# Recurrence outputs with high and low part side by side, and earlier sums in the down projection, in a two-block transformer kernel

## What is computed

```
def hgrn2_recurrence(q, k, v, log_f):
    """S_t = diag(f_t) S_{t-1} + k_t v_t^T,  o_t = S_t^T q_t, chunkwise."""
    ...
    q_in = q * jnp.exp(b)
    ...
    scores = jnp.einsum('nbhtk,nbhsk->nbhts', q_in, k_in)
    scores = jnp.where(causal, scores, 0.0)
    o_intra = jnp.einsum('nbhts,nbhsv->nbhtv', scores, v)
    def step(state, inp):
        o_inter = jnp.einsum('bhtk,bhkv->bhtv', q_n, state)
    ...
    o = o_intra + o_inter
...
    o = rms_norm_2(o, hg_norm_g)
    o = o * jax.nn.silu(hz).reshape(B, S, HG_HEADS, HG_DIM)
```

## Time and profile before

| what | value |
|---|---|
| three runs | 1290.31, 1290.8, 1291.3 us; median 1290.8 |
| the profiled execution, its own time | 1290.74 us |
| its span in the profile | 1288.9 us |
| PE busy | 1279.2 us (99%), 6297 matmuls |
| DVE, ACT, POOL busy | 726.0, 689.4, 498.9 us |
| granted clock of PE | 0.999 over the span |
| DMA | 132.32 MB, 103 GB/s on average |

### The profile page before, as it was taken

One profiled execution on the slowest core, in us unless ns is written; L12 is line 12 of the kernel. 1 busy time (PEld: TensorE's weight loads), 2 busy tenths in 40 slices (PEclk: granted clock), 3 DMA queues, 4 the chain that ended last, 5 costly groups with the idle time before them and its releaser, 6 DMA issues.

```text
span 1288.9 us, 16219 instructions
## 1 busy us (share of the span) xinstructions
PE 1279.2 (99%) x6297; PEld 1073.6 (83%) x6297; DVE 726.0 (56%) x1321; ACT 689.4 (53%) x1031; POOL 498.9 (39%) x207
## 2 busy tenths in 40 slices
PE   9999999999999999999999999999999999999998
PEld 7888888888887888888888888888878888888886
DVE  6656556552138456565768377777656556642442
ACT  5535544543235657666447577777655545462422
POOL 4553433434444332322335534434333333334530
PEclk9999999999999999999999999999999999999999
DMA  5732332324332232332243322222223222225411
GB/s 176 274 119 95 91 98 86 103 87 164 98 101 95 86 105 69 98 97 65 66 160 99 115 82 66 82 82 66 82 82 101 72 88 74 91 99 204 163 57 66
DMA packets 42589, 132.32 MB, mean 103 GB/s; under 512 B 6992, under 2 KB 9744, under 8 KB 42000
## 3 DMA queue, kind: packets, MB, share of 16 engines
q1 hardware_dynamic: 36416, 115.36, 28.0%
q10 hardware_dynamic: 6096, 15.92, 3.5%
HBM read 124.97 MB, written 10.49 MB: 105 GB/s over the span
## 4 chain that ended last, share of the span: by engine, by line
PE 93%; DVE 4%; ACT 1%; DMA 1%; issue 1%; POOL 0%; SPq 0%; DVEq 0%; ACTq 0%
PE banks L509 28%; PE banks L511 28%; PE banks L510 28%; PE banks L716 2%; PE banks L708 1%; PE banks L697 1%; DVE ylo L1748 1%; DMA raw<-w 1%; PE banks L623 1%; PE banks L936 1%; DVE nfull L1744 1%; ACT whi L1097 0%; PE banks L968 0%; PE banks L967 0%; DVE acc L1612 0%
## 5 line engine op out<-in xcount | busy, mean ns | idle before, releaser
L499 POOL TENSOR_TENSOR wlo<-raw,whi 128x1024 fp32r<-128x1024 f32 (+2 forms) x198 | 487.9, 2466 | 718.2 <-ACT whi L1097 717.8
L509 PE MATMUL banks<-hhi,whi 128*128 128x512 f32 x736 | 292.9, 398 | 0.2 <-DVE hlo L1795 0.2
L511 PE MATMUL banks<-hlo,whi 128*128 128x512 f32 x736 | 287.2, 390 | 0.0
L510 PE MATMUL banks<-hhi,wlo 128*128 128x512 f32 x736 | 287.1, 390 | 0.0
L1097 ACT ACTIVATE whi<-raw 128x1024 fp32r<-128x1024 f32 (+2 forms) x198 | 205.3, 1038 | 148.8 <-PE banks L511 86.7
L509 PE MATMUL banks<-yhi,whi 128*128 128x512 f32 x464 | 182.8, 394 | 0.7 <-ACT mcg L1471 0.5
L511 PE MATMUL banks<-ylo,whi 128*128 128x512 f32 x464 | 180.9, 390 | 0.0
L510 PE MATMUL banks<-yhi,wlo 128*128 128x512 f32 x464 | 180.7, 389 | 0.0
L511 PEld LDWEIGHTS banks<-hlo,whi 128*128 128x128 f32 x736 | 138.2, 188 | 29.3
L509 PEld LDWEIGHTS banks<-hhi,whi 128*128 128x128 f32 x736 | 138.5, 188 | 25.4 <-DVE hlo L1795 1.0
L510 PEld LDWEIGHTS banks<-hhi,wlo 128*128 128x128 f32 x736 | 138.6, 188 | 24.5
(11 more groups left out here) (389 smaller groups left out, 2177.4 us busy)
## 6 DMA issues: line engine op xcount, KB each, us to landing
raw<-w SPq DMA_DIRECT2D x193, 512.0 KB, 3.5
rel_tab<-relx ACTq DMA_DIRECT2D x1, 4096.0 KB, 19.5
tab<-rel_tab SPq DMA_DIRECT2D x16, 224.0 KB, 3.5
x<-xt ACTq DMA_DIRECT2D x1, 2048.0 KB, 8.7
x_kept<-x ACTq DMA_DIRECT2D x1, 2048.0 KB, 7.4
parts_kept<-mcg SPq DMA_DIRECT2D x8, 256.0 KB, 4.3
mgt<-parts_kept SPq DMA_DIRECT2D x8, 256.0 KB, 3.7
x<-x_kept ACTq DMA_DIRECT2D x1, 2048.0 KB, 8.3
```

The source lines that it names most:

```text
L499: nc.gpsimd.tensor_tensor(lo[:, begin:width], raw[:, n % 2, begin:width], f32(hi[:, begin:width]), ALU.subtract).then_inc(lo_done, 1)
L509: nc.tensor.matmul(dst, a[0], b[0], start=first, stop=False)
L510: nc.tensor.matmul(dst, a[1], b[0], start=False, stop=False)
L511: return nc.tensor.matmul(dst, a[0], b[1], start=False, stop=last)
```

## The change

In the recurrence's outputs the moving operand gets both parts: `hss` and `hqbs` hold for each block 128 high and beside them 128 low columns. A product with the high part of the stationary operand now moves 256 columns, one with the low part 128. An output block so has 256 columns of PSUM, the low-part product apart from the rest; the four blocks take bank 3 and bank 5. New steps add the two up: on ACT `hg_low` copies the low columns (two instructions, 128x256) into `hb`, a tile that is free then, and on DVE `hg_sum` adds the high columns to it (two instructions). What read bank 3 reads `hb`. As bank 5 is taken until `sum`, the score blocks come in the order 1, second half of 3, 0 (behind a wait for `sum`), first half of 3 and 2.

In the down projection the banks are dealt anew, the squares of tiles 0 to 2 stand before `hg_root(7)` on ACT, the others behind it; `down_sums` is laid between the tiles of `dn 5` instead of `g0 0`, and DVE's rotation comes after the means, half of it after the diagonal matrix.

```
-DN_BANK = (1, 0, 2, 5, 4)
+DN_BANK = (1, 0, 2, 4, 6)
...
-            hqbs = [sb(n, [P, 2, TT - 1, P], F32R, scope) for n in ("hqbhi", "hqblo")]
+            hqbs = sb("hqbs", [P, 2, TT - 1, 2, P], F32R, scope)
...
-            hss = [sb(n, [P, S], F32R, scope) for n in ("hshi", "hslo")]
+            hss = sb("hss", [P, TT, 2, P], F32R, scope)
...
+        out_pairs = [bank[3 if t < 2 else 5][:, (t % 2) * 2 * P:(t % 2 + 1) * 2 * P] for t in range(TT)]
+        out_split = [bank[b].rearrange("p (t c v) -> p t c v", c=2, v=P) for b in (3, 5)]
+        hb_parts = [hb[:, i * 2 * P:(i + 1) * 2 * P].rearrange("p (t v) -> p t v", v=P) for i in range(2)]
...
# PE
+                if k == 4:
+                    pe.wait_ge(hpV.sem, hpV.at("qlo", s))
+                    if s >= 1:
+                        pe.wait_ge(htV.sem, htV.at("far1", s - 1))
+                    hg_block(s, 1)
+                if k == 5:
+                    hg_block(s, 3, slice(CROSS, CROSS + P))
+                if k == 6:
+                    if s >= 1:
+                        pe.wait_ge(hoV.sem, hoV.at("sum", s - 1))
+                    hg_block(s, 0)
+                if k == 7:
+                    hg_block(s, 3, slice(0, CROSS))
+                    if s >= 1:
+                        pe.wait_ge(mzA.sem, mzA.at("z", s - 1))
+                    hg_block(s, 2).then_inc(htP.did("scores"), 1)
...
-                last = mm3(bank[3][:, cols], [u[:, s, t, :] for u in hv], [u[:, cols] for u in hss], True, t == 0)
+                nc.tensor.matmul(to, hv[0][:, s, t, :], hss[:, t, :, :], start=True, stop=False)
+                last = nc.tensor.matmul(to[:, 0:P], hv[1][:, s, t, :], hss[:, t, 0, :], start=False, stop=t == 0)
...
+                    nc.tensor.matmul(to, hsts[0][:, t - 1, :], hqbs[:, s % 2, t - 1, :, :], start=False, stop=False)
+                    last = nc.tensor.matmul(to[:, 0:P], hsts[1][:, t - 1, :], hqbs[:, s % 2, t - 1, 0, :], start=False,
+                                            stop=True)
...
+            def down_sums(k):
+                if k not in (2, 3, 6, 7):
+                    return
...
+                if k == 6:
+                    pe.wait_ge(dnV.sem, dnV.at("k1"))
...
+            slab("dn", 5, bank[5], h, between=down_sums)
...
# ACT
+            def hg_low(u):
+                act.wait_ge(htP.sem, htP.at("o", u))
+                act.wait_ge(hpV.sem, hpV.at("four", min(u + 1, HH - 1)))
+                if u >= 1:
+                    act.wait_ge(hoV.sem, hoV.at("norm", u - 1))
+                for got, to in zip(out_split, hb_parts):
+                    low = nc.scalar.activation(to, got[:, :, 1, :], ACT.Copy)
+                low.then_inc(hoA.did("low"), 1)
...
-                act.wait_ge(htP.sem, htP.at("o", u))
-                nc.scalar.activation(ho[:, 0, :], bank[3], ACT.Square).then_inc(hoA.did("sq"), 1)
+                act.wait_ge(hoV.sem, hoV.at("sum", u))
+                nc.scalar.activation(ho[:, 0, :], hb[:, :], ACT.Square).then_inc(hoA.did("sq"), 1)
...
                 if u >= 0:
+                    hg_low(u)
+                cut()
+                if u >= 0:
                     hg_square(u)
-                cut()
...
# DVE
+            def hg_sum(u):
+                dve.wait_ge(hoA.sem, hoA.at("low", u))
+                for got, to in zip(out_split, hb_parts):
+                    last = V.tensor_tensor(to, got[:, :, 0, :], to, ALU.add)
+                last.then_inc(hoV.did("sum"), 1)
...
+                if r >= 1:
+                    hg_sum(r - 1)
                 dve.wait_ge(hpA.sem, hpA.at("qbhi", r))
...
+            down_add("k1", QL, QL + 1)
...
             dve.wait_ge(dnP.sem, dnP.at("tok"))
...
             V.reciprocal(rt3[:, 1, :, :], rt3[:, 0, :, :]).then_inc(dnV.did("inv"), 1)
+            V.tensor_tensor(mt1[:, 0, :], bank[5], mm[:, 1, :], ALU.mult).then_inc(dnV.did("turn"), 1)
+            crossed(dnV, bank[5], (0, 1))
...
                             ALU.mult).then_inc(dnV.did("diag"), 1)
+            crossed(dnV, bank[5], (2, 3))
+            turned_sum(dnV)
```

More of the change, by code:

```diff
@@ L380, in build @@
         hoP = steps("ho_pe", ["ms"], HH)
-        hoA = steps("ho_act", ["sq", "sqhi", "ln", "root"], HH)
-        hoV = steps("ho_dve", ["sqlo", "norm", "y", "yhi", "ylo"], HH)
+        hoA = steps("ho_act", ["low", "sq", "sqhi", "ln", "root"], HH)
+        hoV = steps("ho_dve", ["sum", "sqlo", "norm", "y", "yhi", "ylo"], HH)
         mzA = steps("mz_act", ["z"], HH)
@@ L842, in hg_outputs @@
                     return
[L843 to L844 removed]
+                t, to = k // 2, out_pairs[k // 2]
                 if t == 0:
@@ L895, in _ @@
             slab("dn", 2, bank[2], h, between=lambda k: hg_outputs(s, k))
-            slab("dn", 3, bank[5], h)
+            slab("dn", 3, bank[4], h)
             hg_square(s)
-            slab("dn", 4, bank[4], h)
-            pe.wait_ge(hoV.sem, hoV.at("norm", s))
-            slab("dn", 5, bank[3], h)
+            slab("dn", 4, bank[6], h)
+            def down_sums(k):
+                if k not in (2, 3, 6, 7):
+                    return
+                g, first = k // 4, 2 * (k % 2)
+                if k == 2:
+                    pe.wait_ge(hoA.sem, hoA.at("ln", s))
+                    pe.wait_ge(dnV.sem, dnV.at("q2"))
+                if k == 6:
+                    pe.wait_ge(dnV.sem, dnV.at("k1"))
+                for b in (first, first + 1):
+                    tok = nc.tensor.matmul(bank[3][:, g * TT + b:g * TT + b + 1], dsq[:, (0, QL)[g], b * P:(b + 1) * P],
+                                           ones[:, 0:1], start=True, stop=True)
+                if k == 7:
+                    tok.then_inc(dnP.did("tok"), 1)
+            slab("dn", 5, bank[5], h, between=down_sums)
             def ml_project(r):
@@ L969, in ml_scores @@
                 last.then_inc(msP.did("s"), 1)
[L971 to L983, removed]
             pe.wait_ge(mzA.sem, mzA.all())
-            slab("g0", 0, bank[7], h, between=down_sums)
+            slab("g0", 0, bank[7], h)
             pe.wait_ge(dnV.sem, dnV.at("diag"))
-            for g, b in enumerate((6, 3)):
-                wide = nc.tensor.matmul(bank[b], ones, ddiag[:, g, :], start=True, stop=True)
-            wide.then_inc(dnP.did("wide"), 1)
+            nc.tensor.matmul(bank[3], ones, ddiag[:, 0, :], start=True, stop=True)
+            pe.wait_ge(dnV.sem, dnV.at("sum"))
+            nc.tensor.matmul(bank[5], ones, ddiag[:, 1, :], start=True, stop=True).then_inc(dnP.did("wide"), 1)
             pe.wait_ge(mcA.sem, mcA.at("gate", 0))
```

75 lines of the change are left out of this document (33 added, 42 removed).

## The result

The changed kernel takes 1294.72 us (median of 8 runs, 1293.83 to 1297.24), the kernel before 1290.85 us (median of 8 runs beside them, 1290.26 to 1291.48). The ratio is 1.0033, 95% interval 1.0023 to 1.0043. The forecast was 1294.4 us, slower by more than 0.2%.

The account below looks back on a forecast made before the run. PE bounds the kernel before; the change makes a loop of ACT and DVE, 28.7 us a round, bind instead. 1290.74 + 3.3 (recurrence) + 0.4 (down projection) = 1294.4 us, 8-in-10 range 1285.2 to 1296.8.

Parts of the forecast that it names:

- PE's saving: Recurrence output blocks: each product saves 0.10 us, 0.70 us a round, 5.6 us in eight.
- Rival 4: 256 columns cost as much as twice 128, only the 0.7 is lost: 1295.1 us; 0.08 together with Rival 3.
- rival 2: The loop closes nearly where it was, 0.2 us or less a round longer: 1291 to 1292 us; chance 0.14.
- The chain of ACT and DVE: Recurrence loop without PE, from qlo through adds, square and mzg to the next qlo: 27.3 us becomes 28.7.
- PE's two waits: Each recurrence round, PE waits for qlo at k = 4 (some 0.4 us) and mzg at k = 7 (some 0.8).
- No PE wait in them: From the first masked copy to the next qlo, 22.46 us, ACT and DVE never wait for PE.
- Sum over the rounds: Recurrence up to the last hg_square: six times 0.6, plus 0.37, less 0.70, so +3.3 us instead of -5.6.
- The tail: Down projection: sum ends at 964.65 against 964.26, and pa 0 waits for ACT's gate behind it: +0.4 us.
- Rival 3: dn 5: POOL delays DVE's yhi, ylo and k1, PE waits at its sums: 1296.7 us; 0.08 together with Rival 4.
- Rival 1: Recurrence loop stays under 27.42 us, PE stays the bound and keeps 5.6 us less 0.4: 1285.5 us; chance 0.18.

Follow-up runs that it names:

- load_shift: Changed kernel with Ln and Exp from one table and each weight's copy on ACT one slab later; 1286.50 us, ratio to before 0.9968.
- extra_before: Kernel before, with the high part of the square written twice each round (one more ACT copy); 1290.70 us, ratio 0.9998.
- extra_after: Changed kernel, with the high part of the square written twice each round (one more ACT copy); 1299.79 us, ratio 1.0072.
- load_after: Changed kernel with hg_root's Ln and Exp from one table, one table load less a round; 1294.82 us, ratio to before 1.0031.
- shift_only: Changed kernel with one weight's copy dropped in round 0 and added in round 8, so copies handle the slab before; 1293.39 us, ratio to before 1.0023.
- best: load_shift plus hz and mzg ahead of the square and the gate of g0 0 ahead of sum's high part; 1283.82 us, ratio to before 0.9945.
- mz_cut: mz_first with the weight's copy ahead of the forget gate moved behind it; 1298.43 us, ratio to before 1.0055.
- mz_first: Changed kernel with ACT's gates hz and mzg ahead of the square; 1290.77 us, ratio to before 0.9997.
- mz_load_cut: mz_cut with hg_root's Ln and Exp from one table as well; 1289.92 us, ratio to before 0.9994.
- rec_only: Changed kernel with the down projection's order in ACT, DVE and PE put back, the recurrence's change alone; 1294.17 us, ratio to before 1.0024.
- gate_first: Changed kernel with ACT's gate of g0 0 ahead of sum's high part and the weight's copy; 1292.09 us, ratio to before 1.0008.
- load_shift_before: Kernel before with load_shift's two edits on ACT; 1290.69 us, ratio 0.9998.

## Why the prediction was right, point by point

- **PE's saving**: right. From the output block to the second tile behind it there are 1.16 us (795.40 to 796.56) instead of 1.36, so 0.20 for two products, as summed. PE's own pace was forecast at 27.42 a round; `load_shift` runs at 27.44. Rival 4 (256 columns as dear as twice 128) is out, and so is rival 2: a round grew by 0.58 us, not by 0.2 or less.
- **The chain of ACT and DVE**: right to 0.06 us at each step. Counted from `qlo`, the square was due at +1.66 and came at +1.71, the table load at +2.98 and +3.03, the masked copies at +6.25 and +6.30, the next `qlo` at 28.7 and 28.72. `extra_before` and `extra_after` show the slack of 0.75 and its end.
- **PE's two waits**: 0.4 and 0.8 us a round were forecast; by starts PE lost 0.42 and 0.81 to 0.85, in the list of waits less.
- **"No PE wait in them"**, said of the 22.46 us from the masked copies to the next `qlo`: true of the rows, but incomplete as a reason. The prediction named one loop that needs no PE. A second one, through the ring slot, is as long: with the first shortened the rounds stay at 28.70 (`load_after`), with the second shortened at 28.67 (`shift_only`), with both at 27.44 (`load_shift`). It did not change the number, since both loops give the same length. It would have spoiled a forecast for any repair of the first.
- **Sum over the rounds**: +3.3 forecast, +3.3 measured from the first score block to the last `hg_square`, and term by term: six times 0.58 (forecast 0.6), 0.5 for the first wait, ahead of the first `hg_square` (forecast 0.37, put in the last round), less 0.65 in the last round (forecast 0.70).
- **The tail**: +0.4 forecast, +0.65 measured. The means come 2.6 us earlier than in before, counted from the last `hg_square`, not 2.7, and from there to the end of `sum` it takes 5.88 us, not 5.75. The wait for the gate was put at some 1.7 us and is 2.36 in the list, 2.9 by starts; this size was wrong, though the time was not, since the gate comes 3.67 us behind the end of `sum` in both kernels.
- **Rival 3** (`k1` behind POOL) had its mechanism but not its price: beside POOL `yhi` took 2.51 and `ylo` 2.78 us instead of the 0.43 and 0.69 of before, `k1` ended at 959.85, and PE came at 960.20, 0.35 us later, where 0.3 was forecast. In `extra_after` the margin was used up and PE waited 0.2 us for it.
- **Rival 1** (the loop does not close, 1285.5 us) is what `load_shift` makes true by two edits: 1286.5.
- The profiled execution is 5.2 us over before's. 4.0 are explained above, 1.6 are the fall of the clock, which the prediction did not have, and its recurrence started 0.4 earlier. The median is 3.9 above, and the five executions of after whose clock had not fallen have a median of 1294.41: the forecast of 1294.4 is right without help from the clock.

## What to carry to other kernels

Before removing work from the busiest engine, follow the others around one whole round and add up the loop they make without it: if it is as long as what remains for the busiest engine, the saving turns into a wait. When shortening such a loop gains nothing, look for the instruction that now waits instead; a second loop of the same length shows no idle time until the first is shorter, and here it was a wait for a ring slot that any copy one slab later avoids. Put what another engine waits for ahead of what nobody needs yet: `hz` and `mzg` moved up in ACT's queue gave 4.2 us in the rounds, the gate of `g0 0` 2.6 in the tail. The first gained nothing more in the rounds once both loops were short (`best`).

## What the runs showed that was not expected

After PE's 2.36 us without work ahead of `pa 0`, the granted clock fell in some executions. PE in after (windows; us, PE busy and matmuls, granted clock, DMA share, GB/s):

```profile
970.00:972.00 2.00, 0.47 (x2) 1.00 0.00 0
972.00:974.00 2.00, 2.00 (x8) 0.68 0.42 125
974.00:976.00 2.00, 2.00 (x6) 0.50 0.34 137
976.00:978.00 2.00, 2.00 (x9) 0.96 0.00 0
```

In 974 to 976 it stands at 0.50, the level of 1.2 GHz, and 6 matmuls are done instead of 10 or 11. From `pa 0` to the end after takes 322.6 us (1294.1 less 971.53), before 321.0: 1.6 us for it. `mz_cut` and `shift_only` show the same fall behind the same wait; `load_after`, `extra_after`, `mz_first`, `mz_load_cut` and `load_shift` have the wait and no fall. The profiles of before, `rec_only`, `extra_before`, `gate_first` and `best`, with a shorter wait or none there, have none. So this wait, 2.9 us by itself, cost 1.6 more in three of eight profiled executions.

The mean granted clock of an execution is 0.998 or less where its profile shows the fall. It is so in 28 of the 62 executions of the eight kernels with the wait, three of after's eight among them (1295.16, 1295.92 and 1297.24 us; the other five took 1293.83 to 1294.73). It is 0.999 or 1.0 in every execution of before, `rec_only`, `extra_before`, `gate_first`, `best` and `load_shift_before`. `gate_first` is after without the wait, and none of its 11 executions has the fall, so the wait is what makes it possible; what decides whether it comes is not shown. It blurs medians: in `shift_only` the five executions with it have a median of 1294.64, the six without 1293.08.

The second surprise is how small an instruction POOL can hold: DVE's copy of 8 columns, 0.16 us, took 2.37 in `mz_cut`, so this short instruction was no safer beside POOL than the 128x512 of `rest`, held for 2 us.
